# Two-layer hybrid decoder: mLSTM scores released by the key and value copies, the decode's fills ahead of its state loads, one logarithm ahead of a store wait

## The reference, cut to what matters

```python
s = jnp.einsum('bthd,bshd->btsh', qb, kb) * w_intra
num = (jnp.einsum('btsh,bshe->bthe', s, vb)
       + w_inter[..., None] * jnp.einsum('bhed,bthd->bthe', C, qb))
den = jnp.sum(s, axis=2) + w_inter * jnp.einsum('bhd,bthd->bth', n, qb)
h = num / jnp.maximum(jnp.abs(den), jnp.exp(-m_t))[..., None]
...
C_new = w_c[..., None, None] * C + jnp.einsum('bsh,bshe,bshd->bhed', w_s, vb, kb)
...
y = h * lax.rsqrt(jnp.mean(h * h, axis=-1, keepdims=True) + EPS)
```

## Time and profile before

| | |
|---|---|
| median of 3 runs | 2077.83 us (2076.82 to 2077.99) |
| profiled execution | 2077.84 us |
| its span, first to last instruction | 2076.2 us |
| TensorE busy | 2024.2 us, 97% of the span |
| VectorE busy | 1302.4 us, 63% |
| ScalarE busy | 844.0 us, 41% |
| POOL busy | 223.7 us, 11% |
| granted TensorE clock, mean | 0.995 of full speed |

### The profile page before, as it was taken

One profiled execution on the slowest core, in us unless ns is written; L12 is line 12 of the kernel. 1 busy time (PEld: TensorE's weight loads), 2 busy tenths in 40 slices (PEclk: granted clock), 3 DMA queues, 4 the chain that ended last, 5 costly groups with the idle time before them and its releaser, 6 DMA issues.

```text
span 2076.2 us, 38768 instructions
## 1 busy us (share of the span) xinstructions
PE 2024.2 (97%) x15539; PEld 1940.2 (93%) x15539; DVE 1302.4 (63%) x1978; ACT 844.0 (41%) x1209; POOL 223.7 (11%) x364
## 2 busy tenths in 40 slices
PE   7999999999999999999999999999999999999995
PEld 7999999999999999999999999999888888888885
DVE  5564546675554553344654476667788888888887
ACT  4412323443433222233223226434556555555554
POOL 0002331010000000000024311101100000010021
PEclk9999999999999999999999999999999999999998
DMA  5233347567322223322253385634877887787795
GB/s 186 82 105 119 105 149 277 169 185 280 98 92 92 91 92 97 93 89 90 63 165 99 104 292 177 186 122 131 299 257 246 261 260 254 252 262 258 242 307 178
DMA packets 110417, 358.45 MB, mean 173 GB/s; under 512 B 14488, under 2 KB 18656, under 8 KB 110024
## 3 DMA queue, kind: packets, MB, share of 16 engines
q1 hardware_dynamic: 88472, 282.13, 42.1%
q0 software_dynamic: 21824, 74.58, 11.0%
HBM read 309.91 MB, written 47.20 MB: 172 GB/s over the span
## 4 chain that ended last, share of the span: by engine, by line
PE 87%; DVE 4%; issue 3%; DMA 3%; ACT 2%; POOL 0%; ACTq 0%; SPq 0%; DVEq 0%; POOLq 0%
PE ps L2003 54%; PE ps L2339 11%; PE ps L1997 7%; PE ps L2353 5%; PE ps L2341 5%; PE ps L2359 3%; ACT w_hi L860 2%; DVE w_lo L1247 1%; DMA C_s<-Cs 1%; DMA Cs<-ml_C 1%; DMA kb<-mlstm_key_query_rows 1%; DMA raw<-slabs 0%; DVE sq L1578 0%; DVE gsum L1884 0%; PE ps L2262 0%
## 5 line engine op out<-in xcount | busy, mean ns | idle before, releaser
L1247 DVE TENSOR_TENSOR w_lo<-raw,w_hi 128x1024 fp32r<-128x1024 f32 x320 | 395.8, 1237 | 260.3 <-ACT w_hi L860 257.5
L2003 PE MATMUL ps<-h_hi,w_hi 128*128 128x260 f32 x2544 | 524.6, 287 | 16.9 <-DVE h_lo L1256 14.0
L2003 PE MATMUL ps<-h_hi,w_lo 128*128 128x260 f32 x2544 | 513.1, 283 | 0.0
L2003 PE MATMUL ps<-h_lo,w_hi 128*128 128x260 f32 x2544 | 512.1, 283 | 0.0
L860 ACT ACTIVATE w_hi<-raw 128x1024 fp32r<-128x1024 f32 x320 | 335.6, 1053 | 390.8 <-PE ps L2003 383.3
L2003 PEld LDWEIGHTS ps<-h_hi,w_hi 128*128 128x128 f32 x2544 | 395.1, 189 | 22.4 <-DVE w_lo L1247 16.1
L2003 PEld LDWEIGHTS ps<-h_hi,w_lo 128*128 128x128 f32 x2544 | 392.7, 189 | 0.0
L2003 PEld LDWEIGHTS ps<-h_lo,w_hi 128*128 128x128 f32 x2544 | 392.3, 189 | 0.0
L2339 PE MATMUL ps<-hg,w_hi 128*128 128x320 f32 x1408 | 368.8, 345 | 3.5 <-DVE w_lo L1247 2.6
L2341 PE MATMUL ps<-hg,w_lo 128*128 128x160 f32 x1408 | 333.6, 237 | 0.0
L2339 PEld LDWEIGHTS ps<-hg,w_hi 128*128 128x128 f32 x1408 | 264.3, 188 | 14.5 <-DVE w_lo L1247 6.5
(11 more groups left out here) (386 smaller groups left out, 2653.5 us busy)
## 6 DMA issues: line engine op xcount, KB each, us to landing
raw<-slabs SPq DMA_DIRECT2D x321, 512.0 KB, 3.9
raw_more<-slabs SPq DMA_DIRECT2D x175, 512.0 KB, 4.4
gates_kept<-sq SPq DMA_DIRECT2D x64, 260.0 KB, 2.2
gs<-gates_kept POOLq DMA_DIRECT2D x64, 260.0 KB, 3.6
token_slots<-zeros POOLq DMA_DIRECT2D x1, 9600.0 KB, 34.9
Cs<-ml_C POOLq DMA_DIRECT2D x8, 512.0 KB, 6.8
kb<-mlstm_key_query_rows POOLq DMA_DIRECT2D x8, 512.0 KB, 7.4
qb<-mlstm_key_query_rows POOLq DMA_DIRECT2D x8, 512.0 KB, 8.7
```

The lines of the kernel that those rows point to most:

```text
L1247: tt_op(w_lo[:, n % SPL], raw_slab(n), w_hi[:, n % SPL].bitcast(F32), ALU.subtract).then_inc(lo_ready, 1)
L2003: ins = mm(out[:, hf], wgt_part[:, slot, tile], in_part[:, kk, HALF * hf:HALF * (hf + 1)], start=first and not ends and in_part is in_hi, ...
```

## The change

Four edits. (1) On TensorE the first score products wait for "copies" in place of "scol"; the score products count a semaphore of their own, `scores`, and VectorE waits for "scol" and `scores` before it multiplies. (2) ScalarE copies `n_rows` ahead of the last `C_t`, whose count then covers both, and POOL's wait `n_rows_ready` goes. (3) In the decode of heads 1 to 3, VectorE's first fill stands ahead of the wait for `Cs` and of both multiplications, in place of behind them. (4) ScalarE takes a logarithm of one element, written to a bias that this layer has used already, ahead of the wait for the mixers' stores.

```diff
-    ml = Steps(sem("mlstm"), turn=1, copies=2, dm=1, exps=7, scol=1, sc01=1, p01=2, sc23=1, p23=2,
+    ml = Steps(sem("mlstm"), turn=1, copies=2, dm=1, exps=7, scol=1, p01=2, p23=2,
                vw=1, out=1, cst=2, absd=1, maxd=1, rec=1,
                scaled=TT, back=1, h=2)
...
-    n_rows_ready = sem("n_rows_ready")
+    scores = sem("scores")
...
-            pool.wait_ge(n_rows_ready, l + 1)
             pool.dma_start(n_p[l].rearrange("o (h p) -> (o h) p", p=P), n_rows[:]).then_inc(st_nm, 16)
...
                 at("back")
+                if h == H - 1:
+                    nc.scalar.activation(n_rows[:], ps[0:H, 7, P:2 * P], ACT.Copy)
                 nc.scalar.activation(C_t[:, h], ps[:, 7, 0:P], ACT.Copy).then_inc(ml.sem, 1)
-                if h == H - 1:
-                    nc.scalar.activation(n_rows[:], ps[0:H, 7, P:2 * P], ACT.Copy).then_inc(n_rows_ready, 1)
...
                 if t == 1:
+                    nc.scalar.activation(ifb[0:1, l, 0:1], eps[0:1], ACT.Ln)
                     for s, n in mixers_done(l):
                         act.wait_ge(s, n)
...
-                at("sc01")
+                at("scol")
+                dve.wait_ge(scores, 2 * rep + 1)
                 for tt in range(2):
...
-                at("sc23")
+                dve.wait_ge(scores, 2 * rep + 2)
                 for tt in range(2, 4):
...
                 if h > 0:
                     dve.wait_ge(ds.sem, ds.after("h", rep - 1))
+                    fill(2)
                 dve.wait_ge(C_in[b], 16 * (rep // 2 + 1))
                 inc(by_token(C_h, w3b[:, h, NS_TOK:2 * NS_TOK]))
                 dve.wait_ge(kb_in[b], 16 * (rep // 2 + 1))
                 inc(by_token(kb[:, b], vs8[:, h]))
-                if h > 0:
-                    fill(2)
                 at("scaled")
...
-                at("scol")
+                at("copies")
                 for tt in range(2):
                     ins = exact(ps[:, 4 + tt, 0:NP_TOK - tt * P], k[:, h, token_tile(tt)],
                                 q[:, h, tt * P:NP_TOK])
-                ins.then_inc(ml.sem, 1)
+                ins.then_inc(scores, 1)
                 fill(1)
                 at("p01")
                 for tt in range(2, 4):
...
-                ins.then_inc(ml.sem, 1)
+                ins.then_inc(scores, 1)
```

## The result

| | before | after |
|---|---|---|
| median | 2078.70 us (20 runs) | 2069.17 us (20 runs) |
| profiled execution | 2077.84 us | 2069.15 us |
| its span | 2076.2 us | 2067.5 us |

The ratio is 0.9949 [0.9937, 0.9961]: faster, by half a per cent. The profiled executions differ by 8.69 us, where the sum said 8.96.

What follows compares the result with a forecast made beforehand. TensorE, busy 97% of the span, was taken to bound the kernel, so only its stalls could pay. 5.70 + 1.48 + 1.78 = 8.96 us off 2077.84 gave 2068.9 us, range 2066.9 to 2072.7.

Steps and rivals of the forecast that it cites:

- the sum: Whole kernel: 5.70 at the scores plus 1.48 and 1.78 at the head norms, 8.96 us won.
- Scores: Score products of heads 1 and 3: TensorE's stall for VectorE's `vw` copy goes, 2.85 us a layer, 5.70 in all.
- n_rows ahead of C_t: ScalarE's two copies swapped before the decode: costs nothing; without cover at most 0.25 us a layer.
- Fill: VectorE's fill moved ahead of the state in the decode: head 3 ends 0.2 us earlier, layer 1 0.50.
- the walk: Head-by-head timing of layer 0's decode: head 1 ends 0.52 us later, head 2 1.06 earlier, head 3 0.32 earlier.
- Logarithm: Head norm: table load of 1.28 us hidden in the store wait; with the earlier store 1.48 and 1.78 us.
- The margin of the preload: ScalarE before the head norm: load and small logarithm fit the 1.67 us wait with 0.2 us to spare.
- rival (a): Head norm: the table switch takes another 1.28 us and overruns the wait; 6.8 us won, 2071.0 us; chance 0.12.
- Rival (c): Decode: head 3's `Cs` load comes late through a longer store and load chain; slower, up to 2083.9 us; chance 0.03.
- The bound: Low end of the range: all that TensorE loses at these places, 10.2 us, 2067.6; less scatter 2066.9.
- ScalarE's side: Head norm, layer 0: ScalarE's gain of 1.48 us, smaller than TensorE's loss of 1.76, so it counts.
- Signs of being wrong: New TensorE wait at "p01" or the head norm above 1 us a layer, or a wait for head 3's `Cs`.

Runs made afterwards that it cites:

- after_again: The changed kernel run once more, unaltered, as the measure for later kernels; 2069.16 us, ratio 0.9955.
- log_only: The kernel before with only the one-element logarithm put ahead of the store wait; 2075.83 us, ratio 0.9978.
- scores_log: The changed kernel without the moved fill, which stays behind the key product; 2069.51 us, ratio 0.9955.
- fill_head2: The changed kernel with the fill ahead of the state in head 2 only; 2067.89 us, ratio 0.9946.
- fills_only: The kernel before with only the decode's first fill moved ahead of the state; 2077.04 us, ratio 0.9986.

## Why the prediction was right, point by point

**Scores: 5.70 predicted, 5.67 measured.** ScalarE's copy of the pooling product stands ahead of the decode, so it dates this part alone: 293.30 to 290.17 is 3.13, less the 0.31 us by which the stage starts earlier, 2.82 in layer 0; 1188.67 to 1181.26 is 7.41, less 4.56 for the same reason, 2.85 in layer 1. `after_again` gives the same two numbers. That the cost of a stall is read from the chain (5.70) and not from the idle time (4.6) was right. The multiplication by the scores ended 1.60 us ahead of TensorE's half fill; 1.6 was worked out.

**n_rows ahead of C_t: nothing, as said.** ScalarE waits the same 0.46 us ahead of L1004, as it did before. The part was not run by itself.

**Fill: the walk holds in direction and nearly in size.** Against before's times less the 3.13 us that the scores gave, head 1 ends 0.72 us later (0.52 predicted), head 2 0.87 earlier (1.06), head 3 0.14 earlier (0.2). Each head ends 0.2 us later than the walk has it (for head 3 the walk had 0.32, and the forecast took 0.2 of it). The trace of after shows both parts. A head takes 7.78 us from its first multiplication to its end (324.85 to 332.63), 0.12 more than the 7.66 of the walk: the state's sum starts 1.25 us behind the start of the key product (325.99 to 327.24), where the split had started 1.13 behind it (328.37 to 329.50). And VectorE's split starts 1.16 us behind ScalarE's (333.47 to 334.63), not 1.10. In layer 1, which the prediction did not walk by its own rows, head 3 ends 1243.09 - 7.41 - 1235.25 = 0.43 earlier (0.50 predicted).

**Logarithm: 1.48 and 1.78 predicted.** The first one comes 353.13 - 348.54 - 3.13 = 1.46 us earlier in layer 0, and 1248.98 - 1239.81 - 7.41 = 1.76 in layer 1. TensorE's x120 fill comes 4.60 - 3.13 = 1.47 and 9.19 - 7.41 = 1.78 earlier: all of ScalarE's gain reaches TensorE, and no more of TensorE's own loss is won back. In this pair of profiles the agreement with the sum is to 0.02, and that is partly luck. The same reading of `after_again` gives 1.32 and 1.15, in sum 0.79 less than predicted: its store lands 0.14 us later in layer 0, and in layer 1 comes the late load of the queries shown above. Its execution took 2069.19 us all the same, since the rest of it was shorter by nearly as much.

**The margin of the preload** was put at 0.2 us and is 0.55 and 0.73. The step that was short: the walk kept the split ahead of the preload where it stood behind the squares, but with TensorE's stall gone the split's slab is ready when the squares end, and the 0.31 us wait that ScalarE had there is no more. Without the moved fill the margin is 0.21 us and nothing (`log_only`) or 0.21 and 0.35 (`scores_log`), so in a kernel without that edit rival (a) would have been near.

**Rival (c)** had 2.3 us of margin from a chain of store and load of 13.1 us. `fill_head2` dates it at 13.0; in after VectorE asks for head 3's `Cs` at 336.39, which is 336.39 - 321.10 - 13.0 = 2.3 us after it can be there. The price of this rival was put somewhat high: both DMAs at 10.6 us would make the chain 8.7 us longer and not 9.8, for the store and the load in it take 5.32 and 7.15 us in before's chain of waits, where the prediction took the median of 5.7 for both.

**The bound** was the weak place, though nothing in the time shows it. The low end had all that TensorE loses at these places at 10.2 us (2067.6 less the scatter of 0.6 is 2067.0, not the 2066.9 stated), and the forecast took the smaller gain of ScalarE's side as given by the change. `fill_head2` wins 10.33. So ScalarE's side was no fixed limit; it was set by two of the three moved fills. They make heads 1 and 3 wait for a split, and in `scores_log` VectorE waits for a load of `Cs` in head 2 alone.

**Signs of being wrong.** None came: no wait at "p01", 0.24 us a layer at the head norm, and no wait for `Cs` of head 3.

## What to carry to other kernels

Price a stall by what the instructions behind it lose in the chain of waits, and give a gain to the tighter of two waits in a row: one of them mended alone (`fills_only`, 0.40 us) moves the loss to the other. Where filler work is moved ahead of a wait, ask of each instance whether there was a wait to cover; filler that itself waits for another engine only delays the work behind it (both fills ahead of three heads: 11.9 us lost against the changed kernel). When a function table is loaded ahead of a wait, check the time to spare in the version with all other edits, since they move both ends of it.

## What was not expected of the hardware

Two function switches in a row on ScalarE take 1.48 us each: the load of 1.28 and the small function of 0.20, with no gap between the rows. A stall of TensorE of 4.35 us was followed by 3.8 us at half the granted clock (0.50), and the work behind it took 2.2 us more than in after; the stalls of 1.4 and 0.9 us at the scores, at a clock of 1.00, cost about 0.3 more than their idle time (1.77 us for the score products instead of 1.50). VectorE's split in head 1 takes 2.34 us where the one in the decode takes 1.23, before and after alike; what does that was not tried.
